# Two of every six expert weight fills are asked for by ScalarE's DMA queue

## The reference, cut to what matters

```python
logits = (xt @ w_router + b_router)          # 256 tokens, 32 experts
top_v, top_e = lax.top_k(logits, 4)          # each token goes to 4 of them
gate = softmax(top_v)
# for each expert e and its tokens xb:
gu = xb @ w_gate_up[e] + b_gate_up[e]        # 1024 -> 2048, f32
g, u = gu[:, :1024], gu[:, 1024:]
g = minimum(g, 7.0); u = clip(u, -7.0, 7.0)
hmid = (u + 1.0) * (g * sigmoid(1.702 * g))
out = hmid @ w_down[e] + b_down[e]           # 1024 -> 1024
y += gate * out                              # back at the tokens' rows
```

## Time and profile before

| | us |
|---|---|
| median of 3 runs | 1210.96 (1210.92 to 1211.49) |
| profiled execution | 1210.22 |
| its span in the trace | 1208.5 |
| PE busy | 1123.5 (93%) |
| DVE, ACT, POOL busy | 320.0, 234.1, 36.3 |
| q1 (SP's queue) | 444.37 MB, 88.3% of the DMA engines' time |
| q10 (ACT's queue) | 0.30 MB, 0.2% |

### The profile page before, as it was taken

One profiled execution on the slowest core, in us unless ns is written; L12 is line 12 of the kernel. 1 busy time (PEld: TensorE's weight loads), 2 busy tenths in 40 slices (PEclk: granted clock), 3 DMA queues, 4 the chain that ended last, 5 costly groups with the idle time before them and its releaser, 6 DMA issues.

```text
span 1208.5 us, 12834 instructions
## 1 busy us (share of the span) xinstructions
PE 1123.5 (93%) x5458; PEld 500.3 (41%) x5459; DVE 320.0 (26%) x718; ACT 234.1 (19%) x464; POOL 36.3 (3%) x34
## 2 busy tenths in 40 slices
PE   6999989999999999999999999899999998999896
PEld 5886666754333333333333333333333333333332
DVE  4777665213222111111221111111111111111111
ACT  5674565432000000000100000000000000000002
POOL 0000050040000000000000000000000000000000
PEclk9999999999999999999999999999999999999999
DMA  8823433848999999999999999999999999999995
GB/s 350 306 89 144 136 140 138 318 175 339 427 429 426 427 428 427 428 426 428 428 427 427 428 427 429 427 427 428 427 429 425 428 428 428 427 428 427 427 428 214
DMA packets 44299, 445.50 MB, mean 369 GB/s; under 512 B 6065, under 2 KB 10257, under 8 KB 19441
## 3 DMA queue, kind: packets, MB, share of 16 engines
q1 hardware_dynamic: 42096, 444.37, 88.3%
q10 hardware_dynamic: 2144, 0.30, 0.2%
HBM read 443.60 MB, written 1.05 MB: 368 GB/s over the span
## 4 chain that ended last, share of the span: by engine, by line
PE 55%; DMA 37%; DVE 5%; ACT 3%; issue 1%; SPq 0%; DVEq 0%; ACTq 0%
DMA R<-in_w_gate_up 21%; PE ps L2006 17%; PE ps L2015 13%; DMA XM<-in_w_gate_up 7%; PE ps L2035 4%; PE ps L1520 4%; DMA XMT<-in_w_gate_up 3%; DMA R<-in_w_down 3%; PE ps L1982 3%; PE ps L1540 3%; PE ps L1542 3%; PE ps L1541 3%; PE ps L1880 2%; PE ps L1774 1%; PE ps L1997 1%; DMA A<-in_w_xkv 1%
## 5 line engine op out<-in xcount | busy, mean ns | idle before, releaser
L2006 PE MATMUL ps<-R,convT 128*64 128x512 f32 x1248 | 277.1, 594 | 23.5 <-DMA R<-in_w_gate_up 23.4
L1423 DVE TENSOR_SCALAR A<-ps 128x512 f32<-128x512 f32 x30 | 20.8, 692 | 648.5 <-PE ps L2006 648.5
L2006 PEld LDWEIGHTS ps<-R,convT 128*64 128x64 f32 x1248 | 86.6, 137 | 202.3 <-issue 152.0
L2015 PE MATMUL ps<-R,A 128*64 128x512 f32 x608 | 133.9, 592 | 1.3 <-DMA R<-in_w_down 1.3
L910 ACT ACTIVATE A<-A 128x512 f32<-128x512 f32 x30 | 18.9, 630 | 474.3 <-DVE A L1423 474.3
L2015 PEld LDWEIGHTS ps<-R,A 128*64 128x64 f32 x608 | 42.9, 137 | 80.3 <-issue 78.9
L2035 PE MATMUL ps<-A,convT 64*128 64x512 f32 x248 | 61.6, 615 | 0.7 <-ACT A L917 0.7
L1982 PE MATMUL ps<-H,convT 128*64 128x512 f32 x256 | 60.4, 593 | 0.3 <-DVE convT L1378 0.3
L917 ACT COPY A<-ps 128x512 f32<-128x512 f32 x30 | 17.6, 585 | 221.4 <-PE ps L2015 221.4
L2006 PE MATMUL ps<-QK,convT 128*64 128x512 f32 x208 | 48.2, 606 | 2.8 <-DMA QK<-in_w_gate_up 2.8
L2006 PE MATMUL ps<-XM,convT 128*64 128x512 f32 x208 | 47.0, 594 | 3.7 <-DMA XM<-in_w_gate_up 3.7
(11 more groups left out here) (322 smaller groups left out, 1248.6 us busy)
## 6 DMA issues: line engine op xcount, KB each, us to landing
R<-in_w_gate_up SPq DMA_DIRECT2D x78, 2048.0 KB, 40.8
R<-in_w_down SPq DMA_DIRECT2D x37, 2048.0 KB, 41.9
QK<-in_w_gate_up SPq DMA_DIRECT2D x13, 2048.0 KB, 40.9
XM<-in_w_gate_up SPq DMA_DIRECT2D x13, 2048.0 KB, 42.4
A<-in_w_gate_up SPq DMA_DIRECT2D x12, 2048.0 KB, 40.7
XMT<-in_w_gate_up SPq DMA_DIRECT2D x12, 2048.0 KB, 42.2
A<-in_w_down SPq DMA_DIRECT2D x7, 2048.0 KB, 42.6
XMT<-in_w_down SPq DMA_DIRECT2D x7, 2048.0 KB, 44.1
```

What stands on the lines that cost most here:

```text
L1423: V.tensor_scalar(gcl, bank(G_BANK), LIM, None, ALU.min).then_inc(m_gcl, 1)
L2006: last = mm(bank(b)[s * SLOTS:(s + 1) * SLOTS, :], xg[:, 4 * (j % 2) + 2 * c + j // 2, :], w[:, c * 2 * FF + at + s * BANK:c * 2 * FF + at ...
L2015: last = mm(bank(o)[s * SLOTS:(s + 1) * SLOTS, :], h[:, c, i * SLOTS:(i + 1) * SLOTS], w[:, c * D + s * BANK:c * D + (s + 1) * BANK], star ...
```

## The change

The helper `fill` takes the queue as an argument. `behind(k, j)` names the fill n = 6k + j + 9, the one whose slot is free when `freed` reaches 6k + j. SP leaves out the fills in `SECOND`, which are n = 6k + 13 and n = 6k + 15 as far as they are below 180; ACT asks for them on its own queue. It does so right after the sigmoid of expert k (j = 4, waiting for `freed` >= 6k + 4) and right after the copy to `orow` (j = 6, waiting for `freed` >= 6k + 6). The fill, its slot and its arrival semaphore are the same as before. The fills 0 to 12, 14 and all from 178 on stay with SP.

```diff
@@ -409,6 +409,22 @@
+        def fill(queue, e, j, slot):
+            if j < GU_FILLS:
+                src = w_gate_up[0, e, j * 2 * P:(j + 1) * 2 * P, :].rearrange("o (p c) n -> p (o c n)", c=2)
+            else:
+                f = (j - GU_FILLS) * 4 * P
+                src = w_down[0, e, f:f + 4 * P, :].rearrange("o (p c) n -> p (o c n)", c=4)
+            return queue.dma_start(ring[slot], src)
+
+        def behind(k, j):
+            n = FILLS * k + j + RING - 1
+            return n if n < FILLS * A_EXP else None
+
+        SECOND = [behind(k, j) for k in range(A_EXP) for j in (GU_FILLS, FILLS)]
@@ -464,16 +480,9 @@
                 for n, (k, j) in enumerate(STREAM):
+                    if n in SECOND:
+                        continue
...
-                        fill(slice(k, k + 1), j, ring_slot(k, j)).then_inc(arrived[ring_slot(k, j)], 16)
+                        fill(sp, slice(k, k + 1), j, ring_slot(k, j)).then_inc(arrived[ring_slot(k, j)], 16)
@@ -905,9 +914,17 @@
+                def second_fill(k, j):
+                    n = behind(k, j)
+                    if n is not None:
+                        act.wait_ge(freed, FILLS * k + j)
+                        e, i = STREAM[n]
+                        fill(act, slice(e, e + 1), i, ring_slot(e, i)).then_inc(arrived[ring_slot(e, i)], 16)
+
                 def expert(k):
                     act.wait_ge(m_gcl, k + 1)
                     nc.scalar.activation(sgm, gcl, ACT.Sigmoid, scale=ALPHA).then_inc(m_sg, 1)
+                    second_fill(k, GU_FILLS)
                     if k + 1 < E:
                         act.wait_ge(m_gath, k + 2)
                         nc.scalar.copy(hmf, bank(X_BANK)).then_inc(m_xr, 1)
@@ -915,6 +932,7 @@
                     act.wait_ge(freed, FILLS * (k + 1))
                     nc.scalar.copy(orow, bank(O_BANK)).then_inc(m_o, 1)
+                    second_fill(k, FILLS)
```

More of the change, by code:

```diff
@@ L486, in _ @@
                                             sp.wait_ge(g_freed, r * (E * FILLS) + e * FILLS + i + 1)
-                                            fill(bass.ds(e, 1), i, spare_slot(i)).then_inc(g_arr[i % SPARE], 16)
+                                            fill(sp, bass.ds(e, 1), i, spare_slot(i)).then_inc(g_arr[i % SPARE], 16)
                             sp.wait_ge(g_done, 1)
```

## The result

The changed kernel takes 1214.95 us (median of 7 runs, 1213.48 to 1216.78) against 1210.91 us of the kernel before in the same comparison: ratio 1.0038, 95% interval 1.0026 to 1.0049, so 4.0 us slower. The forecast was 1216.8 us, +5.8.

A forecast was written before the change was run, and what follows sets the result against it. The DMA stream (29.4 us per expert against PE's 26.91) was taken as the bound; 12.7 us of later starts less 6.9 given back made +5.8, so 1216.8 us, range 1207 to 1240.

The forecast's parts named there:

- The bound and the rate: Expert stage: the DMA stream sets the pace and stays at 427 to 428 GB/s after the change.
- Rival C: Expert stream: two queues raise the rate above 430 GB/s, 9 us off for each 1%; 1199 to 1208 us, chance 0.12.
- rival B: Expert stream: turns between queues cost rate, 0.19 us per packet or a tenth; 1220 to 1300 us, chance 0.18.
- Issue and waits: ScalarE in each expert: the added issues, 0.35 us each, fit its idle time and its waits cost nothing; taken as 0.
- The upper bound of 4 us: Experts 28 and 29: a long issue could delay the copy of gathered rows and hold PE 2.0 us in each.
- Turns, and landing out of order: Expert stream: engines serve both queues in turn, so ScalarE's fills land 10 to 14 us after being asked for.
- The lag: Steady part of the experts: PE starts each expert 12.7 us later than before, paid once, from around expert 8.
- a sum of PE's waits 6 us larger: Sign for the reordering forecast: PE's waits on DMA move to j=0 and j=2 and their sum grows about 6 us.
- What is given back: After the last moved fill, 177: PE regains 2.45 us each in experts 28 and 29 and tail waits, 6.9 us.
- my upper bound: Net about +9 us if fill 170 is waited for another 2 us and ScalarE's queue gets more than its half.
- the tail: Before the last down projections: PE regains its waits of 0.66 and 1.35 us.

The follow-up runs named there:

- bounds 168 and 174: The changed kernel with ScalarE asking only for fills below 168 or below 174 instead of 180: 1210.84 us (ratio 1.0004) and 1214.06 us (ratio 1.0034).

## Why the prediction was right

**The bound and the rate.** Right. 427 to 428 GB/s and a share of 1.01 with one queue and with two. Rival C (a higher rate) and rival B (a lower one) didn't happen for fills of 16 KB runs. Something like B exists with small loads on the second queue, 9.6 and 12.1 us, but not as the price for each packet that B worked with: the load with two packets per engine cost no less than the one with nine.

**Issue and waits, taken at 0.** Right, but not for the reason given: an issue takes 0.335 us on ScalarE (at most 0.351), and it doesn't fill the 0.36 us of idle time before the copy but runs beside the sigmoid (1082.31 to 1082.65, the sigmoid to 1082.93). PE's wait for ScalarE is unchanged at 13.7 us. The upper bound of 4 us, for late copies in experts 28 and 29, had no ground in the change itself: ScalarE asks for nothing in these two, its last issue is at 1094.3 us.

**Turns, and landing out of order.** Right, and now shown: 14 us to landing (10 to 14 were estimated), packets one for one while both queues are loaded, of equal size (66 and 69) and of unequal (97 and 101, 93 and 92), and 36 to 37 us when ScalarE's queue needs all of its turns. The Trainium skill, "DMA: Bandwidth & Descriptors", section "Queues, rings and completion order", says that engines go round the queues by packet. These counts agree. In the same page of the Trainium skill the section "Issuing engines are not separate DMA queues" says that DMAs of several issuers interleave and that only issue time is saved. The traces agree on the rate, 427 to 428 GB/s, and add that the order of landing changes, and with it the time.

**The lag.** 12.7 us forecast, 11.9 at expert 28 (12.3 if one counts from the first expert fill, which PE takes up 0.4 us earlier in this execution). The step holds; the waits at j=0 and j=2 are there, from about 532 us on (the forecast said near 500). What I named as its sign, a sum of PE's waits 6 us larger, did not show: 38.1 us against 38.0. From 285 us on PE is instead busy 4.0 us longer, with matmuls at half clock behind the longer waits, and the forecast had no term for the clock.

**What is given back.** Sign and mechanism right, split wrong. Expert 28 gave back 1.3 us and not 2.45, because it still waited for fill 170; that was in my upper bound, but not in the value taken. Expert 29 and the tail gave back 6.5 us (10.55 to 4.01) and not 4.45: expert 29 its 2.45, and the tail 4.1 instead of 2.0. I had taken the tail from the idle times of the earlier trace rows alone. But in the profiled run of before PE takes 4.87 us for fill 184, which takes 3.63 in the changed kernel, and the four short matmuls ahead of it take 1.06 us instead of 0.62. The rows of before, which the earlier trace rows begins behind, and the stretch from 1164 us:

```profile
1163.64 1.06 PE L1997 MATMUL ps<-A,MK 96*64 96x512 bf16 x4 [0.71 <-DVE convT L1498]
1164.47 4.87 PE L2006 MATMUL ps<-QK,convT 128*64 128x512 f32 x16
...
1164.00:1167.00 3.00, 3.00 (x10) 1.05 (x8) 0.01 (x1) 0.00 (x0) 0.00 (x0) 0.50 1.01 431
```

The granted clock is at its half level (0.50) there, and 1.6 us of lag go at this place (8.10 us of lag ahead of it, at the transposes, 6.46 behind it). This doesn't mean that the kernel before lost time to the clock: PE waits for two fills after it, 0.66 and 1.35 us, so the stream set its time, and the slow matmuls stand where it would have waited. The run with only 6k+13 moved bears this out: it takes fill 184 in 3.63 us and yet takes up the last fill at 1195.54, against 1195.47 before. What PE could gain in the tail was this slack too, not only the idle time. The other 0.4 us are in the two waits themselves, which held PE up by 0.8 and 1.6 us, where its idle times are 0.66 and 1.35 (the last but one fill, 1189.97, starts 5.01 us after the one ahead of it, in the changed kernel 3.44). So 12.7 - 6.9 became 11.9 - 7.85, and +5.8 became +4.0. That the two misses of the give-back, -1.1 and +2.1 us, partly cancel is luck.

**The size of one expert's give-back.** I treated 2.45 us per expert as even. It is an average: the runs with bounds 168 and 174 show a step of 4.6 us, and the next one, to 180, about 0.6 us.

## What to carry to other kernels

Here a second DMA queue next to a full one added no bandwidth; it changed which bytes come first. Fills that jump a deep queue push back the ones that the consumer waits for. The lag is the number of fills that lie landed ahead, times a fill's time, less the slack of the fill that is waited for now: with two moved fills 3 x 4.90 us less 2.0 us makes 12.7 (11.9 measured), with only 6k+13 moved 2 x 4.90 less 2.0 makes 7.8 (7.6 measured). It costs nothing if the consumer has slack left after the last of them to work it off, so judge it by what remains of the stream, and count from there. Count as slack not only the consumer's idle time but also work that ran slowly ahead of a wait. And give each queue the share of the bytes that its turns will carry if the order of need is to be kept.

## What the runs showed of the hardware that was not expected

- Turns between the two queues went by packet and regardless of its length: with both loaded 93 packets of up to 16 KB against 92 of up to 8 KB in 5 us, 1.52 and 0.67 MB; with the sizes the other way round 97 against 101.
- An issue on ScalarE ran beside its sigmoid: it began 0.01 us after it, took 0.34 us, and delayed nothing.
- Runs of 8 KB in all of SP's fills, with twice as many DMAs, lowered the stream from 427 to 423 GB/s; in ScalarE's third of the bytes alone, to 425.
- 56 loads of 16 KB on the second queue cost 9.6 and 12.1 us (424 and 423 GB/s), with 2 packets per engine no less than with 9. Not explained.
- PE's granted clock came to its half level at some of the single waits for a fill of 1.9 to 4.1 us, and at none of up to 1.8 us; at some long ones it stayed at full (one of 3.7 us in the run with ScalarE's fills halved). In the changed kernel the stretch from 540 to 600 us has 0.97 (the table of stretches above), in the kernel before both stretches of the earlier trace rows have 1.00. A second place is fill 184 in the tail, behind idle times of 0.69, 0.46 and 0.71 us between short matmuls: the clock fell there in the profiled executions of before and of four other runs, and held in the other eight. While the stream is the bound this is hidden (the place after the wait of 3.27 us); after the last wait nothing hides it, as in the runs with only 6k+15 moved and with bound 174.
